# Cross attention in one block, its input pieces staged in buffers of their own, panel loads between the others, closing products beside the last softmax

## The reference

```python
merged = jax.nn.sigmoid(gate_a) * o_a + jax.nn.sigmoid(gate_b) * o_b
x = x + merged @ w_out[l]
x = x + memory_cross_attention(rmsnorm(x, cross_norm[l]), rmsnorm(mem, mem_norm[l]),
                               w_cq[l], w_ckv[l], w_co[l])
...
def memory_cross_attention(h, m, w_cq, w_ckv, w_co):
    q = (h @ w_cq).reshape(b, s, X_HEADS, X_HEAD_DIM)
    mk, mv = _split(m @ w_ckv, (D_MODEL, D_MODEL))
    scores = jnp.einsum('bshd,bmhd->bhsm', q, mk) * (X_HEAD_DIM ** -0.5)
    probs = jax.nn.softmax(scores, axis=-1)
    out = jnp.einsum('bhsm,bmhd->bshd', probs, mv).reshape(b, s, D_MODEL)
    return out @ w_co
```

## Time and profile before

| | before |
|---|---|
| median of 3 runs (lowest, highest) | 3278.09 us (3276.77, 3279.98) |
| profiled execution, its time and its span | 3278.38 us, 3276.6 us |
| TensorE busy | 2956.0 us, 90% |
| VectorE, ScalarE, GpSimd busy | 1630.8, 1087.6, 1361.2 us |
| granted clock over the run | 0.955 of 2.4 GHz |

### The profile page before, as it was taken

One profiled execution on the slowest core, in us unless ns is written; L12 is line 12 of the kernel. 1 busy time (PEld: TensorE's weight loads), 2 busy tenths in 40 slices (PEclk: granted clock), 3 DMA queues, 4 the chain that ended last, 5 costly groups with the idle time before them and its releaser, 6 DMA issues. The chain is left out here.

```text
span 3276.6 us, 61778 instructions
## 1 busy us (share of the span) xinstructions
PE 2956.0 (90%) x26984; PEld 2423.5 (74%) x26984; DVE 1630.8 (50%) x1764; ACT 1087.6 (33%) x1780; POOL 1361.2 (42%) x708
## 2 busy tenths in 40 slices
PE   3899999996899999999999998688986799999995
PEld 2688888884677887778787877566764688887885
DVE  6654444444166655656665565143223744553445
ACT  2433333223243333434343443232222333333221
POOL 1344444443255444545554455352131344444441
PEclk7999999997999999999999999899987899999997
DMA  3232224433321111222211122421012222234441
GB/s 140 76 101 81 77 107 159 147 128 106 123 60 53 58 51 46 66 77 61 63 55 46 46 77 79 146 77 45 13 32 84 68 78 78 88 111 148 145 145 67
DMA packets 260168, 279.10 MB, mean 85 GB/s; under 512 B 13504, under 2 KB 213312, under 8 KB 257728
## 3 DMA queue, kind: packets, MB, share of 16 engines
q1 hardware_dynamic: 259904, 275.20, 25.6%
HBM read 224.83 MB, written 50.33 MB: 84 GB/s over the span
## 5 line engine op out<-in xcount | busy, mean ns | idle before, releaser
L483 POOL TENSOR_TENSOR w_low<-ffn_work,w_high 128x1024 fp32r<-128x1024 f32 x182 | 445.1, 2446 | 668.9 <-ACT w_high L556 394.6
L523 PE MATMUL bank<-h_high,w_high 128*128 128x512 f32 x1232 | 485.1, 394 | 57.4 <-DVE h_low L667 34.3
L523 PE MATMUL bank<-h_low,w_high 128*128 128x512 f32 x1232 | 483.5, 392 | 0.0
L523 PE MATMUL bank<-h_high,w_low 128*128 128x512 f32 x1232 | 483.1, 392 | 0.0
L1204 POOL TENSOR_TENSOR mix_panel_low<-arena,mix_panel_high 128x1024 fp32r<-128x1024 f32 x114 | 276.1, 2422 | 413.1 <-ACT mix_panel_high L1581 413.1
L1307 PE MATMUL bank<-mix_h_high,mix_panel_high 128*128 128x512 f32 (+1 forms) x896 | 358.2, 400 | 25.3 <-POOL mix_panel_low L1204 14.9
L1307 PE MATMUL bank<-mix_h_low,mix_panel_high 128*128 128x512 f32 (+1 forms) x896 | 343.2, 383 | 0.0
L1307 PE MATMUL bank<-mix_h_high,mix_panel_low 128*128 128x512 f32 (+1 forms) x896 | 342.1, 382 | 0.0
L714 DVE TENSOR_TENSOR h_low<-ffn_work,h_high 128x512 fp32r<-128x512 f32 x88 | 205.5, 2335 | 250.5 <-ACT h_high L571 250.5
L523 PEld LDWEIGHTS bank<-h_high,w_high 128*128 128x128 f32 x1232 | 233.9, 190 | 110.4 <-issue 59.7
L540 PE MATMUL bank<-h_high,w_high 128*128 128x512 f32 x704 | 275.1, 391 | 4.3 <-DVE h_low L714 4.3
(11 more groups left out here) (299 smaller groups left out, 5817.5 us busy)
## 6 DMA issues: line engine op xcount, KB each, us to landing
arena<-w_in SPq DMA_DIRECT2D x96, 512.0 KB, 3.8
ffn_work<-w_down SPq DMA_DIRECT2D x88, 512.0 KB, 3.7
a_spill<-ffn_work SPq DMA_DIRECT2D x88, 256.0 KB, 2.3
ffn_work<-a_spill SPq DMA_DIRECT2D x88, 256.0 KB, 2.6
ffn_work<-w_gate SPq DMA_DIRECT2D x12, 1024.0 KB, 5.6
ffn_work<-w_up SPq DMA_DIRECT2D x12, 1024.0 KB, 8.1
arena<-w_gate SPq DMA_DIRECT2D x10, 1024.0 KB, 5.5
arena<-w_up SPq DMA_DIRECT2D x10, 1024.0 KB, 8.0
```

The costliest lines, as they stand in the source:

```text
L483: nc.gpsimd.tensor_tensor(slot(w[1], q), src, slot(w[0], q).bitcast(F32), ALU.subtract).then_inc(s_low, 1)
L523: last = mm(bank[:, bk, :], w[wp][:, q % RING, kt, e], h[hp][:, k, kt], start=fresh and kt + wp + hp == 0, stop=kt == KT // 2 - 1 and wp = ...
```

## The change

The mixer: the last unit list is dealt anew, so that the first point of `prepare(15)` is empty, and two units instead of one stand in `prepare(17)`. The four pieces of the merged half no longer pass the `raw` slots; they go into `staged`, the buffers of `prob` and `prob_t`. Pieces 2 and 3 of the tensor are loaded at the end of solve 15, rounded by ScalarE and lowered by VectorE (`lower_piece`) inside solve 16; pieces 0 and 1 follow when those are done and are rounded after the last unit. The wait for the last merged writes and the clearing of the mixer's semaphores move into SyncE's stream of the next block; the semaphores of the stage before the mixer are cleared in the mixer. Cross attention becomes one block. Its value transposes stand behind product 1, in banks 4 to 7. Transfers alternate with panel loads. Source tiles are split two at a time at first, and the first half's norm is scaled two tiles at a time beside products 9 to 14. In the last head, TensorE forms the first four tiles' terms of closing products 0 and 1 (banks 4 to 7) before it waits for the probabilities; the output of that head goes to banks 0 to 3.

```diff
--- before.py
+++ after.py
...
-            def act_high(self, act):
+            def act_high(self, act, tiles=range(KT)):
...
-            def pool_low(self, pool):
+            def pool_low(self, pool, tiles=range(0, KT, 2)):
...
-            def dve_scale(self, dve, ready=None):
+            def dve_scale(self, dve, ready=None, tiles=range(KT)):
...
-            KV, OUT, SRC = UNITS, UNITS + 2 * KT, UNITS + 2 * KT + 2
-            ALL = SRC + KT // 2
+            KV, OUT = UNITS, UNITS + 2 * KT
+            ALL = OUT + 2
...
-                if i <= ITER:
+                if i < ITER - 1:
                     return [NP * (i + 1) + j for j in range(NP - 1)]
-                return list(range(NP * (ITER + 1) + NP - 1 + 4, OUT))
+                if i == ITER - 1:
+                    return [None] + [KV + j for j in range(NP - 2)]
+                if i == ITER:
+                    return [KV + NP - 1 + j for j in range(NP - 1)]
+                return [OUT - 2, OUT - 1]
...
-                return [NP * (i + 2) - 1] if i < ITER else list(range(NP * (ITER + 2) - 1, NP * (ITER + 2) + 3))
+                if i < ITER - 1:
+                    return [NP * (i + 2) - 1]
+                return [KV + NP - 2] if i == ITER - 1 else list(range(OUT - 6, OUT - 2))
...
+            PIECES = (2, 3, 0, 1)
...
+            staged = [t.rearrange("p a b -> p (a b)").rearrange("p (a b) -> p a b", b=HALF) for t in (prob, prob_t)]
...
+                    def load_piece(q):
+                        if q < 2:
+                            sp.wait_ge(S("xt_added"), 2 * len(LEVELS) * ITER)
                         else:
-                            if unit == SRC:
-                                for j in range(2):
-                                    sp.wait_ge(s_mw[j], 16 * (PAIRS // 2))
-                            k = 2 * (unit - SRC)
-                            src = m_spill.rearrange("p (k t) -> p k t", t=T)[:, k:k + 2, 0:HALF]
-                            dst = raw[unit % 2].rearrange("p a b -> p (a b)").rearrange("p (a b) -> p a b", b=HALF)
-                        sp.dma_start(dst, src).then_inc(s_raw[unit % 2], 16)
+                            sp.wait_ge(S("piece_low"), q - 1)
...
+                        k = 2 * PIECES[q]
+                        sp.dma_start(staged[q % 2],
+                                     m_spill.rearrange("p (k t) -> p k t", t=T)[:, k:k + 2, 0:HALF]).then_inc(
+                                         s_piece[q % 2], 16)
...
+                    for used in shared_used:
+                        sp.sem_clear(used)
...
+                        if i == ITER:
+                            load_piece(0)
+                            load_piece(1)
                         load(NP * (i + 1) + 2)
+                        if i > ITER:
+                            load_piece(2)
+                            load_piece(3)
...
-                    for unit in range(NP * (ITER + 2) + NP + 2, ALL):
-                        load(unit)
-                    for j in range(2):
-                        sp.wait_ge(s_mw[j], 16 * PAIRS)
...
+                    pool.wait_ge(S("piece_high"), 3)
+                    k = 2 * PIECES[2]
+                    G.tensor_tensor(hA[1][:, k:k + 2], staged[0], hA[0][:, k:k + 2].bitcast(F32),
+                                    ALU.subtract).then_inc(S("piece_low"), 1)
...
+                    def round_piece(q):
+                        act.wait_ge(s_piece[q % 2], 16 * (q // 2 + 1))
+                        act.wait_ge(S("proj_ready"), UNITS if q < 2 else OUT)
+                        k = 2 * PIECES[q]
+                        A(hA[0][:, k:k + 2], staged[q % 2], ACT.Copy).then_inc(S("piece_high"), 1)
...
+                                    elif not live and u < 2 and first == 3:
+                                        round_piece(u)
...
+                    def lower_piece(q):
+                        dve.wait_ge(S("piece_high"), q + 1)
+                        dve.wait_ge(S("piece_low"), q)
...
+                                if not live and n in (2, 4):
+                                    lower_piece(n // 2 - 1)
...
-            with nc.Block() as block:
-                @block.sync
-                def _(sp):
-                    for used in sems.values():
-                        sp.sem_clear(used)
+                    lower_piece(3)
+                    dve.wait_ge(S("piece_low"), 4)
...
                     for j in range(2):
-                        sp.dma_start(oT[:, 4 * j:4 * j + 4, HALF:T],
-                                     m_view[:, 4 * j:4 * j + 4, HALF:T]).then_inc(s_merged[j], 16)
-                    for j in range(2):
-                        load_x(1, j)
-                    for k in range(4, Q + 2):
+                        sp.wait_ge(s_mw[j], 16 * PAIRS)
+                    load_merged(0)
+                    for used in mixer_sems:
+                        sp.sem_clear(used)
+                    load(sp, 4)
+                    load_merged(1)
+                    load(sp, 5)
+                    load_x(1, 0)
+                    load(sp, 6)
+                    load_x(1, 1)
+                    for k in range(7, Q + 2):
+                        load(sp, k)
+                    with sp.Fori(1, XH) as i:
+                        for t in range(2):
+                            sp.wait_ge(s_wlow, i * 2 + (Q + t - 3))
+                            sp.dma_start(raw[t][:], wq[:, :, t * P:][:, :, ds(i * NMEM, P)]).then_inc(s_pan[t], 16)
+                    for k in range(CO, CO + KT):
                         load(sp, k)
...
+                    def out_part(o, first, end):
+                        for kt in range(first, end):
+                            for n in range(2):
+                                if o == 0:
+                                    pe.wait_ge(s_slow, KT + 2 * kt + n + 1)
+                                last = terms(2 * ((o + 2) % 4) + n, o % 2, n, kt, kt + 1)
+                        return last
...
+                        else:
+                            for o in range(2):
+                                panel_ready(pe, CO + o)
+                                out_part(o, 0, 4)
...
+                    for k in range(Q):
+                        project_out(k)
+                        if k == 1:
+                            turn_values()
+                        elif k == KT:
+                            pe.wait_ge(s_vst, 4)
+                            nx[0].pe_sums(pe)
+                        elif k == KT + 1:
+                            nx[0].pe_scale(pe)
                     project_first()
-                    with pe.Fori(0, XH - 1) as i:
+                    pe.wait_ge(s_padd, Q)
+                    with pe.Fori(0, LAST - 1) as i:
                         head(i, False)
-                    head(XH - 1, True)
+                    head(LAST - 1, False)
+                    head(LAST, True)
+                    for first, end in ((4, 6), (6, 8)):
+                        for o in range(2):
+                            last = out_part(o, first, end)
+                            if end == KT:
+                                last.then_inc(s_ready, 1)
+                    for o in range(2, KT):
+                        panel_ready(pe, CO + o)
+                        if o < 4:
+                            pe.wait_ge(s_os, 2 * XH + 2)
+                        else:
+                            pe.wait_ge(s_padd, Q + o - 3)
+                        out_part(o, 0, KT).then_inc(s_ready, 1)
...
+                    done = 0
+                    for k in range(2, Q + 2):
+                        if k == KT + 2:
+                            nx[0].pool_root(pool)
+                        subtract_low(pool, k % 2, k)
+                        if 4 <= k < KT + 2:
+                            for _ in range(2 if k < 6 else 1):
+                                subtract_source(pool, 1, done, done + 1)
+                                done += 1
+                        if KT + 3 <= k < KT + 7:
+                            nx[0].pool_low(pool, [2 * (k - KT - 3)])
...
+                    done = 0
+                    for k in range(2, Q + 2):
+                        round_high(act, k % 2, k, k // 2)
+                        if k == 3:
+                            store_values()
+                        if 4 <= k < KT + 2:
+                            for _ in range(2 if k < 6 else 1):
+                                if done % 4 == 0:
+                                    act.wait_ge(s_merged[done // 4], 16)
+                                round_source(act, 1, done)
+                                done += 1
+                        if KT + 3 <= k < KT + 7:
+                            nx[0].act_high(act, range(2 * (k - KT - 3), 2 * (k - KT - 2)))
+                        square(k - 2)
...
+                    exp(LAST - 1)
+                    next_q(LAST - 1)
+                    store_probs(LAST - 1)
+                    act.wait_ge(s_ready, CO)
```

(21 more changed lines are left out.)

320 lines of the change are left out of this document (119 added, 201 removed).

## The result

The changed kernel took 3228.11 us (median of 4 runs, 3226.34 to 3230.97) against 3277.43 us in the runs beside it. The ratio is 0.9849, with a 95% interval of 0.9832 to 0.9866. The profiled execution took 3226.34 us with a span of 3224.6, 52.0 less than the span before. The four runs fall in two pairs, near 3226.4 and near 3230.4; the four of c_after do not (3228.0 to 3228.6, and 3231.5). A part of this text is about differences of this size.

A forecast was written before the change was run, and what follows sets the result against it. TensorE is busy for 90% of the span, so only its waits and low-clock stretches can pay. 2.5 - 0.5 + 9.9 + 6.6 + 3.1 + 9.0 - 1.0 + 4.6 + 14.9 = 49.1 us off 3278.4 gives 3229.3, range 3223 to 3234.

The forecast's parts named there:

- (a): Preparation of iteration 15: memory keys' units start one point later, so the root comes sooner; 2.5 us gained (0 to 5).
- (g): Before the heads: no change of block, so the second half's sums start sooner; 4.6 us gained (2.6 to 5.5).
- (b): Pieces staged early, loaded ahead of a panel near solve 16: 0.5 us lost (0 to 2), splitting steps free.
- (c): End of the mixer to the output products: first product starts 14.0 us sooner, less 2.2 and 1.9; net 9.9 gained.
- Rival B: Mixer's end gives only part: queue order puts another 4 us on the root, (a) is nothing; 3238 to 3241, chance 0.12.
- (d): Output products: panel 4's load goes between the others, removing a 3.7 us wait and 2.9 after it; 6.6 us gained.
- (e): Output products: source pieces split two at a time shorten the wait at product 8; 3.1 us gained (2 to 3.9).
- (f): First half's norm spread over products 9 to 14: panel 12's delay goes, 9.0 us gained, 1 lost (0 to 8).
- Rival A: Port shared by VectorE and GpSimd makes the spread norm late, 7 us more than taken: 3236, chance 0.2.
- My rule that each wait brings a cold stretch: On TensorE, a wait costs its own length and some 3 us behind it, mostly at 1.2 in place of 2.4 GHz.
- (h): Last head: closing products fill the 12.0 us softmax wait, a change of block goes; 14.9 us gained (11 to 17).
- Rivals C and D: C: closing sources late, softmax wait stays, 3239, chance 0.05. D: panels late, clock falls each unit, 3313, chance 0.03.

The follow-up runs named there:

- c_after: The changed kernel once more, unedited, as yardstick: 3228.57 us, ratio 0.9858 to the kernel before.
- u_point: Changed kernel with the empty point of iteration 15 put last instead of first: 3224.62 us, ratio 0.9848.
- i_point: Changed kernel with second-half norm sums 12 matmuls later, root ahead of the last split, and iteration 15's empty point last: 3216.49 us, ratio 0.9814.
- u_pieces: Changed kernel with the first two staged pieces loaded behind the fourth panel of iteration 16, not ahead of the first: 3228.89 us, ratio 0.9852.
- u_clears: Changed kernel with the mixer's semaphores cleared in a block of their own ahead of cross attention: 3233.86 us, ratio 0.9873.
- i_sums: Changed kernel with the second half's norm sums on TensorE placed 12 matmuls later: 3224.09 us, ratio 0.9834.
- u_head: Changed kernel with no closing products beside the last softmax; products 0 and 1 run whole after the head: 3238.89 us, ratio 0.9891.
- u_norm: Changed kernel with the first half's norm scaled in one stretch again: 3233.08 us, ratio 0.9871.
- u_loads: Changed kernel with both merged halves and both x loads ahead of panel 4: 3232.12 us, ratio 0.9866.

## Why the prediction was right, step by step

The forecast was 3229.3 us and the medians are 3228.11 and 3228.57, inside its own range; all the marks named for it were met. The first output product came at 2091.88 (near 2093 forecast), no wait over 2 us in the sixteen products, clock 1.00 from product 1 on to 2190, 0.8 us before the last transposes (under 1.5), the last closing add at 2450.4 (near 2452). That the whole fits to about 1 us is in part luck. (a) and (g) came 3.2 us short together and (b) 2.95 us better; the chain and the heads gave 2.5 us in this profile that no step had promised, and c_after has -0.7 and 0.05 there.

**(a) was priced at the wrong mark.** I took the root and the merge as the path; the merge did come 2.5 us earlier (34.71 to 32.18 us), as the term says. But TensorE's own path gained 0.75, or 1.0 over the kernels with the point first (67.2 in the mean of eleven, against 68.2). u_point and i_point, where the transfer wait is restored, have 68.25 and 66.08, the same 67.2 in the mean, so the removed wait does not show as the reason. The unit that left is the likely one, untested. Whether the place of the point itself costs time is not settled: the medians with it last are 3.5 to 5.3 us lower in two pairs, the ratio of the first pair is not.

**(b) failed in sign.** I saw the queue order correctly, that the pieces' loads delay a panel, and charged 0.5 us. I did not ask what the late panel's split would no longer collide with. It collided with the merge step, which is worth 2.45 us (u_pieces). The four steps in the chain cost nothing, as taken: the chain follows the clock alone.

**(c) held**, 12.4 us against 11.8, and so did its inner working: the root started 4.2 us later against the chain's end where 4.0 was charged. Rival B's mark (over 4 us) was thereby met, but that loss was already in the sum and no other came on top. u_clears has 6.0 us in place of 0.5 at the handover, 5.5 apart, where I had deduced 5.6 in place of 0.5.

**(d), (e), (f)** gave 16.3 us with (c)'s transposes against 15.8. One by one, undone, they are 6.3 (6.6 predicted), 2.5 (3.1) and 8.7 (8.0 net). Rival A's lock is real, but inside the products it lies on VectorE's lows, and no wait of TensorE there ends on it. Where it did cost TensorE time is behind them, in (g).

**(g) gave 3.1 of 4.6.** The sums did come 4.8 us sooner, but a 1.4 us wait stayed, for the last square's add that a split holds to 2.45 us, and behind it came the stretch at 0.79 that cost 1.6. My rule that each wait brings a cold stretch was applied to waits that left, not to those that stayed. i_sums takes both away.

**(h) held**, 15.5 against 14.9: 11.5 is the gap filled (u_head), 4.1 the rest, by subtraction. Rivals C and D did not occur.

What stays open: whether and why the empty point's place matters. In both profiles with it last the chain of 16 ran at clock 1.00 (26.96 us), and in two of eleven with it first (u_clears and i_sums, which do not touch the mixer's order). That fits a preference or an accident; it was not settled. Nor was it settled why the medians of u_norm and u_loads rose by 4.5 and 3.5 us where their stages lost 8.7 and 6.3.

## What to carry to other kernels

Price a step at the instruction that the busiest engine waits for next, not at the value that it makes ready; a removed wait can be refilled by the ones behind it, as in (a). When a change delays a transfer, follow it to the split that it feeds and to what that split holds up: a later one can be a gain, as in (b). And when the sum is made, look at the short waits that remain on TensorE too, since taking away one of 1.4 us here gave 1.8 us, and 3.4 where a cold stretch had followed it.

## What the runs showed of the hardware

**The same gap sometimes costs a cold stretch and sometimes not.** Ahead of the chain of 16 TensorE idles 1.8 us in u_point and 2.0 in the changed kernel; the clock behind it is 1.00 in the one and 0.72 in the other (fences of u_point; 2.0 is in the first list of waits above), and 0.57 in c_after behind 1.9 us. Behind the 4.59 us of u_pieces it is 0.50, and behind the same 4.59 us 0.64 in the kernel before. The gap is 1.8 to 2.0 us in all twelve profiles that load the pieces first; in eight of them the clock falls to 0.50 within 2 us of the chain's start and stays there for 7 to 10 us, in four it does not fall. The chain then takes 26.96, 29.8, 31.2 or 32.4 us (30.5 before). The heads show it in small. Three heads of TensorE, changed kernel: window, length, busy, granted clock.

```profile
2225.72:2265.80 40.08, 37.76 (x161) 1.00 0.09 27
...
2305.87:2347.50 41.63, 39.45 (x161) 0.96 0.09 26
```

The same of c_after:

```profile
2229.29:2271.09 41.80, 39.48 (x161) 0.96 0.09 25
2271.09:2312.85 41.76, 39.44 (x161) 0.96 0.09 26
2312.85:2352.78 39.93, 37.75 (x161) 1.00 0.09 27
```

A head is 40.0 us at the full clock and 41.6 to 41.8 with one fall in it, while the waits inside the heads are alike in both profiles (the longest, for ScalarE's copy, is 2.3 us). In the fourteen profiles one, two or all three of these heads had a fall, with no edit there. Steps of 1.6 us here and of 1.3 to 2.8 in the chain, two or three together, are of the size by which runs of the changed kernel differ (3226.3 to 3231.5), though most of those runs have no profile. This is why stages, not medians, had to settle the small terms.

*TensorE: Matmul & The Clock Gate* of the Trainium skill, section "Part 1: The HAM clock gate", says that the measurement that sets the clock runs freely and does not start anew with the kernel, so that the point at which the clock changes depends on the phase. The levels in the table agree with that, and no run here tests it by itself.
